# First SwiGLU's up projection in quads of seven quarter products, modulation rows moved behind it

## The reference

```python
for i in range(2):
    sh1, sc1, g1, sh2, sc2, g2 = ada_params(c, ada_w[i], ada_b[i])   # silu(c) @ w + b, six vectors of 1024
    ax = rms_norm(hx, norm_mix[i]) * (1 + sc1) + sh1
    yx = retention_mixer(...) if i == 0 else conv_mixer(ax, conv_w_in, conv_w, conv_w_out)
    hx = hx + g1 * yx
    fx = rms_norm(hx, norm_ffn[i]) * (1 + sc2) + sh2
    hx = hx + g2 * ((silu(fx @ w1[i]) * (fx @ w3[i])) @ w2[i])       # w1, w3: 1024 x 2816; w2: 2816 x 1024
return rms_norm(hx, final_norm)
```

## Time and profile before

| | us |
|---|---|
| median of 3 runs | 2257.63 (2257.34 to 2257.82) |
| the profiled execution | 2258.87 |
| its span | 2257.1 |
| mean granted clock of TensorE in the span | 0.998 of full |
| TensorE busy | 2239.3 (99%) |
| VectorE / ScalarE / GpSimd busy | 1483.9 / 868.9 / 232.3 |
| DMA: bytes moved, mean rate | 326.10 MB, 144 GB/s |

### The profile page before, as it was taken

How to read it: one execution, slowest core, us unless ns; L and a number is a source line. 1 busy time by engine, 2 the same in 40 slices (tenths; PEclk the granted TensorE clock), 3 DMA queues, 4 the chain that set the end, 5 groups by cost and what they waited for, 6 DMA issues and landing times.

```text
span 2257.1 us, 31951 instructions
## 1 busy us (share of the span) xinstructions
PE 2239.3 (99%) x11632; PEld 1906.4 (84%) x11632; DVE 1483.9 (66%) x2287; ACT 868.9 (38%) x1248; POOL 232.3 (10%) x187
## 2 busy tenths in 40 slices
PE   9999999999999999999999999999999999999998
PEld 4888888888888898888888878888889889999987
DVE  5558766689999866755746467665436446777622
ACT  4534442355554343313233244323224223554422
POOL 0000000036674001011110100100000000000000
PEclk9999999999999999999999999999999999999999
DMA  8442115423324628475765657876432332555421
GB/s 316 159 131 74 58 61 186 149 66 103 101 93 148 221 71 236 116 191 146 181 170 139 177 132 221 254 232 195 149 103 72 106 101 68 177 183 182 159 94 56
DMA packets 90939, 326.10 MB, mean 144 GB/s; under 512 B 10064, under 2 KB 10960, under 8 KB 89680
## 3 DMA queue, kind: packets, MB, share of 16 engines
q1 hardware_dynamic: 58432, 213.90, 28.5%
q10 hardware_dynamic: 19440, 72.96, 9.9%
q0 software_dynamic: 12960, 37.75, 8.4%
HBM read 322.48 MB, written 39.85 MB: 161 GB/s over the span
## 4 chain that ended last, share of the span: by engine, by line
PE 94%; DVE 3%; issue 1%; DMA 1%; ACT 1%; SPq 0%; DVEq 0%
PE bank L493 81%; PE bank L1015 8%; PE bank L1490 1%; DMA res<-in_x 1%; DVE rstd L680 1%; DVE hx_lo L692 0%; PE bank L1572 0%; PE bank L1348 0%; DMA w_raw<-in_wstream 0%; PE bank L1545 0%; DVE w_lo L452 0%; ACT hx_hi L627 0%; DVE tnorm L686 0%; PE bank L1514 0%; ACT w_hi L444 0%
## 5 line engine op out<-in xcount | busy, mean ns | idle before, releaser
L493 PE MATMUL bank<-hx_hi,w_hi 128*128 128x512 f32 (+1 forms) x1648 | 622.1, 377 | 5.3 <-DVE hx_lo L692 4.6
L493 PE MATMUL bank<-hx_hi,w_lo 128*128 128x512 f32 (+1 forms) x1648 | 611.6, 371 | 0.0
L493 PE MATMUL bank<-hx_lo,w_hi 128*128 128x512 f32 (+1 forms) x1648 | 611.6, 371 | 0.0
L452 DVE TENSOR_TENSOR w_lo<-w_raw,w_hi 128x1024 fp32r<-128x1024 f32 x290 | 354.7, 1224 | 343.5 <-ACT w_hi L444 339.7
L444 ACT ACTIVATE w_hi<-w_raw 128x1024 fp32r<-128x1024 f32 x335 | 353.8, 1056 | 426.5 <-PE bank L493 305.6
L493 PEld LDWEIGHTS bank<-hx_hi,w_hi 128*128 128x128 f32 x1648 | 311.2, 189 | 61.7 <-issue 4.9
L493 PEld LDWEIGHTS bank<-hx_hi,w_lo 128*128 128x128 f32 x1648 | 311.1, 189 | 53.2
L493 PEld LDWEIGHTS bank<-hx_lo,w_hi 128*128 128x128 f32 x1648 | 311.3, 189 | 52.8 <-issue 1.4
L2681 DVE SCALAR_TENSOR_TENSOR bank<-zpad,cols,bank 128x512 f32<-128x512 f32 x352 | 232.1, 773 | 4.6 <-ACT bank L2081 4.6
L493 PE MATMUL bank<-hid_hi,w_hi 128*128 128x512 f32 (+1 forms) x594 | 218.5, 368 | 0.0
L493 PE MATMUL bank<-hid_hi,w_lo 128*128 128x512 f32 (+1 forms) x594 | 217.2, 366 | 0.0
(11 more groups left out here) (368 smaller groups left out, 3595.7 us busy)
## 6 DMA issues: line engine op xcount, KB each, us to landing
w_raw<-in_wstream SPq DMA_DIRECT2D x316, 512.0 KB, 3.5
ada_raw<-in_ada_nk ACTq DMA_DIRECT2D x128, 512.0 KB, 4.3
quad_sums<-in_quad_first POOLq DMA_DIRECT2D x36, 512.0 KB, 5.2
ada_raw<-in_wstream SPq DMA_DIRECT2D x25, 512.0 KB, 3.4
w_raw<-quad_sums SPq DMA_DIRECT2D x19, 512.0 KB, 3.8
quad_sums<-in_quad_more POOLq DMA_DIRECT2D x18, 512.0 KB, 7.6
quad_sums<-quad_sums POOLq DMA_DIRECT2D x36, 256.0 KB, 5.6
ada_raw<-quad_sums SPq DMA_DIRECT2D x17, 512.0 KB, 4.0
```

Of the source, the lines that this page charges most:

```text
L452: nc.vector.tensor_tensor(w_lo[nb.at % RING][:], raw_at(nb)[0][:], w_hi[nb.at % RING][:].bitcast(F32), ALU.subtract).then_inc(lo_ready, 1)
L493: ins = nc.tensor.matmul(out_ap, s, m, start=first and at == 0, stop=last and at == n - 1)
```

## The change

The first SwiGLU gets the second's form. Its up projection is now 4 whole tiles and 18 quads: 8 + 63 blocks. The functions of the quads get a number w (0 or 1) of the SwiGLU. GpSimd makes two sets of 90 steps, one behind the other: the first over the 60 blocks from B_RET + 2, the second over 111 blocks from the first quad block on. SP waits for the first set (and rows up to 80) before the first SwiGLU's quads, and for the second before the second's. Modulation rows 81 to 111 move to the first down projection (one or two per block), 112 to 127 to the short conv (two per group of three blocks), with four buffers. t_norm, t_hi and t_lo are laid out anew so that both SwiGLUs can use them.

```diff
-B_SD0 = B_SW0 + 2 * HT
+TILEWISE = 4
+N_QUADS = HT - TILEWISE
+QUAD_BLOCKS = 7 * N_QUADS // 2
+B_QUAD = [B_SW0 + 2 * TILEWISE]
+B_SD0 = B_QUAD[0] + QUAD_BLOCKS
...
+B_QUAD += [B_SW1 + 2 * TILEWISE]
+B_SD1 = B_QUAD[1] + QUAD_BLOCKS
...
+ADA_BEFORE = 81
...
+        for n in range(N_BLOCKS):
+            for w in range(2):
+                if B_QUAD[w] <= n < (B_SD0, N_BLOCKS)[w]:
+                    loads[n] = landing(("raw0", "raw1", "ada0", "ada1")[(n - B_QUAD[w]) % 4], n)
+            if n not in loads:
+                loads[n] = landing("raw%d" % ((n if n < B_SD0 else n - B_SD0) % 2), n)
+            if n == B_SD0:
+                row_loads = {a: landing(("ada1", "ada0", "ada2", "ada3")[(a - ADA_BEFORE) % 4], None) for a in range(ADA_BEFORE, 128)}
...
+            if i is None and a >= ADA_BEFORE:
+                if a >= ADA_BEFORE + 4:
+                    act.wait_ge(ada_done, a - 3)
+                act.dma_start(row_loads[a][0][:], ada_nk[a]).then_inc(row_loads[a][1], 16)
+                return
...
+        ADA_ROWS = [range(ADA_BEFORE + (3 * n) // 2, ADA_BEFORE + (3 * n + 3) // 2) for n in range(HT - 1)]
+        CIN_ROWS = [range(112 + 2 * u, 114 + 2 * u) for u in range(KT)]
...
-        SUMS_FROM, SUMS_OVER = B_RET + 2, (B_SW1 - B_RET - 6) // 2
+        SUMS_FROM, SUMS_OVER = (B_RET + 2, B_QUAD[0]), (B_SW0 - B_RET - 4, B_SW1 - B_QUAD[0] - 6)
...
-            sp.wait_ge(ada_done, 128)
-            sp.wait_ge(summed, 16 * SUMS)
-            for n in range(B_QUAD, N_BLOCKS):
...
+            for w in range(2):
+                plain = B_QUAD[w] - w * 2 * N_QUADS
+                sp.wait_ge(ada_done, (ADA_BEFORE, 128)[w])
+                sp.wait_ge(summed, 16 * SUMS * (w + 1))
+                for n in range(B_QUAD[w], (B_QUAD[1], N_BLOCKS)[w]):
+                    slot, landed, _, previous = loads[n]
+                    if previous is not None:
+                        sp.wait_ge(lo_ready, previous + 1)
...
-            swiglu_pe(pe, B_SW0, JX["sw0"], JY["sw0"], nffn0)
-            hidden_down_pe(pe, B_SD0, JY["sd0"], sw_l[0], 0, nmix1, none)
...
+            swiglu_pe(pe, B_SW0, JX["sw0"], JY["sw0"], nffn0, TILEWISE)
+            quads_pe(0)
+            hidden_down_pe(pe, B_SD0, JY["sd0"], sw_l[0], 0, nmix1, lambda ct: quads_out(0) if ct == 0 else None)
...
-            swiglu_act(act, 0, B_SW0, JX["sw0"], JY["sw0"], 80)
-            down_act(act, B_SD0, JY["sd0"], [(nmix1, None)], lambda n: ada_load(act, 125 + n) if n < 3 else None, none)
...
+            quads_act(0)
+
+            def rows_act(n):
+                if n == 0:
+                    act.wait_ge(block_done, B_SD0)
+                    act.wait_ge(lo_ready, B_SD0)
+                for a in [*(ADA_ROWS[0] if n == 0 else ()), *(ADA_ROWS[n + 1] if n + 1 < len(ADA_ROWS) else CIN_ROWS[0])]:
+                    ada_load(act, a)
+
+            down_act(act, B_SD0, JY["sd0"], [(nmix1, None)], rows_act, none)
...
+                    for a in (CIN_ROWS[4 * i + u + 1] if 4 * i + u + 1 < KT else ()):
+                        ada_load(act, a)
...
+                        if kind < 2:
+                            ada_reduce(dve, CIN_ROWS[4 * i + u][kind], ROW_C2)
...
             def summing(n):
-                pool.wait_ge(block_done, SUMS_FROM + (n * SUMS_OVER) // SUMS)
+                w, m = divmod(n, SUMS)
+                pool.wait_ge(block_done, SUMS_FROM[w] + (m * SUMS_OVER[w]) // SUMS)
                 if n:
                     pool.wait_ge(summed, 16 * n)
 
-            for q in range(N_QUADS):
+            for q in range(2 * N_QUADS):
```

More of the change, by code:

```diff
@@ L427, in raw_at @@
         def raw_at(b):
-            if b.at < B_QUAD:
+            if b.i is not None and not isinstance(b.i, int):
                 return w_raw[b.at % RAW], raw_ready[b.at % RAW], b.loads()
-            n, s = divmod(b.at - B_QUAD, 4)
-            return (quad_raw[s], *((raw_ready[s], 16 * (B_QUAD // RAW + n + 1)) if s < RAW else
-                                   (ada_in[s - RAW], 16 * (128 // 2 + n + 1))))
+            return loads[b.count()][:3]
         def split_hi(act, b):
@@ L1127, in _ @@
                 crow_load(row, crow_landed)
-            with sp.Fori(1, B_QUAD // RAW - 1) as i:
+            with sp.Fori(1, B_QUAD[0] // RAW - 1) as i:
                 for s in range(RAW):
@@ L1763, in _ @@
             swiglu_pe(pe, B_SW1, JX["sw1"], JY["sw1"], nffn1, TILEWISE)
-            for g in range(N_QUADS):
-                quad_pe(pe, g)
-            pe.wait_ge(q_post, OPENED + 4 * N_QUADS - 4)
+            quads_pe(1)
             def out_turn_pe(j):
@@ L2904, in _, with quads_dve, combinations @@
             dve.wait_ge(nffn0.lo, nffn0.tiles + 2 * KT)
-            swiglu_dve(dve, 0, B_SW0, JY["sw0"], 80)
-            modulation(88, COLS["mix"] + 8, 8)
-            down_dve(dve, B_SD0, JY["sd0"], lambda j: ada[:, 72 + j:73 + j], (nmix1,),
-                     lambda n: ada_reduce(dve, 124 + n, ROW_C2) if n < 4 else None)
-            dve.wait_ge(ada_cols, 128)
+            def quads_dve(w):
+                made_sums = sums_dve(dve, w)
+                def combinations(u):
+                    if w == 0 and u == 0:
+                        ada_reduce(dve, ADA_BEFORE - 1, ROW_C2)
+                    if 1 <= u < 4:
+                        next(made_sums)
+                        if u == 2:
+                            next(made_sums)
+                            combined_lo(dve, w, 0, 1)
+                        elif u == 3:
+                            combined_lo(dve, w, 1, 2)
+                            combined_lo(dve, w, 3, 3)
+                swiglu_dve(dve, w, (B_SW0, B_SW1)[w], JY["sw0" if w == 0 else "sw1"], None, TILEWISE, combinations)
+                for u in range(TILEWISE, 4):
+                    combinations(u)
+                for g in range(N_QUADS):
+                    at = list(windows(g))
+                    split_lo(dve, Block(B_QUAD[w] + at[0]))
+                    if g == 0:
+                        combined_lo(dve, w, 2, 4)
+                    else:
+                        quad_hidden_dve(dve, w, g - 1)
+                    split_lo(dve, Block(B_QUAD[w] + at[1]))
+                    if g >= 1:
+                        quad_hidden_lo(dve, w, g - 1)
+                    quad_mid_dve(dve, w, g)
+                    split_lo(dve, Block(B_QUAD[w] + at[2]))
+                    quad_inner_dve(dve, w, g)
+                    for b in at[3:]:
+                        split_lo(dve, Block(B_QUAD[w] + b))
+                    quad_outer_dve(dve, w, g)
+                quad_hidden_dve(dve, w, N_QUADS - 1)
+                quad_hidden_lo(dve, w, N_QUADS - 1)
@@ L2910, in _, with rows_dve @@
+            quads_dve(0)
+            def rows_dve(n):
+                for a in (ADA_ROWS[n] if n < len(ADA_ROWS) else ()):
+                    ada_reduce(dve, a, ROW_C2)
+                if n < len(ADA_ROWS) and 95 in ADA_ROWS[n]:
+                    dve.wait_ge(ada_cols, 96)
+                    modulation(88, COLS["mix"] + 8, 8)
+            down_dve(dve, B_SD0, JY["sd0"], lambda j: ada[:, 72 + j:73 + j], (nmix1,), rows_dve)
+            dve.wait_ge(ada_cols, 112)
             transition_dve(dve, nmix1, lambda j: dve.wait_ge(block_done, B_SD0 + HT),
```

317 lines of the change are left out of this document (155 added, 162 removed).

## The result

The changed kernel takes **2349.55 us** (median of 4 runs, 2341.71 to 2361.84), the one before 2257.73 (4 runs): a ratio of 1.041, 95% interval 1.039 to 1.043. The profiled execution took 2350.55 us with a span of 2348.2. The runs also spread over 20 us where those of before spread over one.

What follows compares the result with a forecast made beforehand. TensorE, busy 99% of the span, was taken as the bound. Matmuls -14.9, stalls +29.5 and +98 and clock +4 sum to +116.6 us on 2258.87, 2375.5 profiled, so a median of 2374 us; range 2310 to 2440.

Steps and rivals of the forecast that it cites:

- matmuls: First SwiGLU: 18 tiles run as quads cost 181.7 us instead of 196.6 on TensorE, -14.9 us.
- first stall: First SwiGLU's quads: set 1 of the sums lands at 1414 us and TensorE waits, +29.5 us.
- short conv: 16 modulation rows move here; VectorE has room, so 0 on TensorE's path.
- second stall: Second SwiGLU's quads: set 2 of the sums lands at 2043 us and TensorE waits, +98 us.
- clock after both stalls: TensorE's granted clock is lowered behind each stall, under 2 us each, +4 us for both.
- rows: 47 modulation rows leave the first SwiGLU for down projection and short conv; 0 on TensorE's path.
- splits: First SwiGLU: VectorE and ScalarE have room for the quads, busy 136 and 93 of 182 us in the second.
- Landing to TensorE in step: At the late quad block, TensorE is back in step 14.4 us after the sums land.
- straight line through the DMA share: Set 2's pace by stage, estimated from DMA share: 38 us a quad in quads, 41 down projection, 37 short conv.
- The sums keep up: No stall if a quad of sums takes under 29.8 us in set 1, 28.5 in set 2; 2243 us, chance 0.05.
- Not slowed by heavier traffic: Sums take 32.1 us a quad everywhere, 22 when quiet; stalls of 26.5 and 39 us, 2312 us, chance 0.2.
- hurting each other: Sums and weight loads slow each other: 42 us a quad in quads, 50 in down projection; 2435 us, chance 0.15.

Runs made afterwards that it cites:

- e1: The changed kernel with all 180 transfers of the sums left out, so the quads multiply with unsummed weights; 2243.68 us, ratio 0.9937.
- e4: The changed kernel with only set 1 of the sums released earlier, in the first block's down projection (717 us instead of 845); 2351.66 us, ratio 1.0411.
- e2: The changed kernel making all the sums, but the quads use unsummed weights and only the kernel's end waits; 2246.77 us, ratio 0.9957.
- e5: The changed kernel without block counts for set 2 of the sums, which starts once set 1 is done; 2346.66 us, ratio 1.0388.
- e7: As e3, but the links that add only copy, so the sums are wrong; 2244.12 us, one run.
- e8: The changed kernel with a quad's two copies in one link (144 links instead of 180), no block counts, released at 718 us; 2251.73 us, ratio 0.997.
- e9: As e8, but released at 845 us as in the change; 2266.75 us, ratio 1.0024.
- e11: As e8, but released at 799 us, behind the modulation loads of the first block's down projection; 2245.96 us, ratio 0.995.
- e3: The changed kernel with sums for two quads at a time, each link two transfers issued together, 90 links instead of 180; 2257.52 us, ratio 0.9998.
- e10: The changed kernel with two quads in one transfer, 72 links of twice the bytes, block counts kept; 2259.80 us, ratio 1.001.

## Why the prediction was right in its sign, and which terms were off

The forecast was two stalls and 2374 us; the two stalls came, and the median is 2349.55. Against e1, which has the change without the wait, the profiled execution of the change divides without a remainder. In e1 the 13th matmul of the first quads (the second product) starts at 1397.39 + 12 x 0.12 = 1398.8 us, that of the second quads at 1928.5.

| step | predicted | measured |
|---|---|---|
| matmuls (span of e1 less that of before) | -14.9 | 2241.1 - 2257.1 = -16.0 |
| first stall | +29.5 | 1415.9 - 1398.8 = +17.0 |
| short conv, rstd to rstd | 0 | 186.3 - 179.6 = +6.7 |
| second stall | +98 | (2033.1 - 1902.7) - (1928.5 - 1876.5) = +78.4 |
| clock after both stalls | +4 | 2 x 2.5 = +5.0 |
| sum | +116.6 | +91.1 (2348.2 - 2257.1) |

**Matmuls, rows, splits: right.** e1 shows both the term and its covers.

**Landing to TensorE in step: right.** I worked out 14.4 us from the splits and the multiply behind the late block; both places show 14.9.

**The first stall was mis-sized by its pace.** The mechanism and place were right. Set 1 landed at 1400.9 us, not 1414: from 845.7 us on, a quad of sums took 30.9 us in the mean of the 18 and 28 us for the last two, where I had 32.1, built from the mean waits of the earlier trace rows and the issues. SP was ready at 1381.1 (1400.9 - 19.8), as forecast. Over 18 quads each 1 us of error in the pace moves the landing by 18 us. And e4 shows that this stall doesn't matter for the end, since the second absorbs it.

**The second stall was mis-sized by the same kind of error.** The estimates by stage against the trace, in us a quad: quads 38 against 37.2 (its first quad took 48.8), down projection 41 against 40.6, transition 32 against 30.2, short conv 37 against 32.6, rest 32 against 28.3, quiet 25 against 26.7. So the straight line through the DMA share held for the two stages that are fullest and overstated the three others, by 1.8 to 4.4 us a quad; the quiet pace was 1.7 us too low. At 1942.7 us 15.2 quads were summed instead of 14.0, and set 2 landed at 2018.2 us, not 2043.

**The short conv was costed at nothing and cost 6.7 us.** I looked at VectorE's room and not at the weight loads, which have two buffers there. Neither the rows nor the traffic alone does it. From rstd to rstd the stage took 179.6 us with no sums (e1) and with them in e2, e4, e5, e7, e8, e9 and e11, 180.4 in e3, 186.3 in the change and 189.7 in e10. Nor do ScalarE's waits for loads decide: in e11 they come to 40.9 us in that stage, and nothing is lost. How the loads fall against the transfers may do it, which no run shows; the cause stays open. For the end it doesn't matter, since without this loss the second stall is as much longer (e5).

**The clock: right within 1 us.** The granted clock was 0.65 in the stretch with the first gap and 0.55 in that with the second, between the levels of 1.2 and 2.4 GHz. In both, TensorE stood idle most of the time. The 1500 matmuls from the second product on took 182.7 us in both places against 180.3 in e1.

**The rivals.** "The sums keep up" failed by 1.1 us a quad in set 1 (30.9 against its threshold of 29.8) and by 5.8 in set 2 (617/18 = 34.3 against 28.5); e11 shows that it was within reach with fewer links and an earlier start. "Not slowed by heavier traffic" (2312 us) is refuted by the 37 to 41 us a quad in the full stages; "hurting each other" (2435 us) by the same pace, where it had 42 and 50, and by quads and a down projection without a gap. In a small way it is true of the short conv, and of the first block's down projection in e8.

## What to carry to other kernels

Work that is hidden must be costed as a chain of its own, by its rate against its due time: the transfers were hidden at one use of them and cost 103 us at two, while GpSimd was busy for 13% of the span. For a serial chain count the links and not only the bytes (3 of 6.9 us here): what doesn't depend on each other goes into one link. The time at which the chain is released was worth more here than its block counts: 46 us earlier gave 21 us (e11 beside e9), set 2 without block counts nothing (e5). Where it can start early, look for what it slows there: beside modulation loads it cost 8.6 us in the first block's down projection (e8) and nothing in that of the first SwiGLU, and both have two buffers for weights.

## What the runs showed of the hardware

- **An accumulating transfer from HBM to HBM takes longer than a copy of the same size.** From issue to landing (medians, beside the other loads), on the page of the change: 512 KB copied 5.2 us, 512 KB added 7.0, 256 KB added 5.2. The fit of the Trainium skill, DMA: Bandwidth & Descriptors, section on the anatomy of one DMA on the SWDGE path, gives estimates of 3.2, 3.2 and 2.6; the measurement decides.

```profile
quad_sums<-in_quad_first POOLq DMA_DIRECT2D x72, 512.0 KB, 5.2
...
quad_sums<-in_quad_more POOLq DMA_DIRECT2D x36, 512.0 KB, 7.0
quad_sums<-quad_sums POOLq DMA_DIRECT2D x72, 256.0 KB, 5.2
```

- **GpSimd's second transfer can be held back without a wait that the profile shows**, by about the landing time of the first: 17 of 18 pairs of 1 MB copies (e10), 12 or 13 of 36 pairs of 512 KB copies (e3, e8, e9, e11), 24 of 54 adding pairs (e3), 8 of 54 where the same pairs only copy (e7). What holds it back was not tested.
- **Landings by queue under load.** In the down projection of the changed kernel, with a DMA share of 0.94, weight loads took 7.7 us in the median, and TensorE still didn't wait; in the short conv, at 0.77, they took 6.2 us, and it did. Before the change they took 3.5 us in the short conv, at 0.33.
- **Kernels with two sets of sums scatter more, whether or not their end hangs on the chain**: 20 us between runs of the change and 22 in e9, where it does, but also 18 us in e10, 9 in e8 and 8 in e2, where it doesn't, against 1 us in the 4 runs of e1 without sums and 2.6 us in the 13 runs of the kernel before beside it.
